# Scan outputs in pairs of heads, and a first modulation in column halves

## The chip, the cores and the metric

One program on one core of a Trainium2 chip. The metric is the device time of one execution in microseconds. The core has five instruction streams that run side by side and meet through semaphores: TensorE (PE; its weight loads are shown apart as PEld), VectorE (DVE), ScalarE (ACT), GpSimd (POOL) and SyncE (SP), which here issues all transfers. Each stream is worked off in the order in which it is written.

## The reference

Batch 1, 512 positions (S), width 1024 (D), float32. A modulated two-layer transformer is followed by a hybrid block with a Mamba-2 scan. Cut to what the change touches:

```python
cond = jax.nn.silu(c)
for i in range(2):
    mod = (cond @ ada_w[i] + ada_b[i])[:, None, :]          # ada_w[i]: 1024 x 6144
    sh1, sc1, g1, sh2, sc2, g2 = jnp.split(mod, 6, axis=-1)
    h = rmsnorm(x, norm1_g[i]) * (1.0 + sc1) + sh1
    y = sliding_window_sink_attention(h, ...)               # i = 0; stick-breaking for i = 1
    x = x + g1 * y
    h = rmsnorm(x, norm2_g[i]) * (1.0 + sc2) + sh2
    x = x + g2 * swiglu(h, w_gate[i], w_up[i], w_down[i])
...
# scan: 4 groups of 8 heads of 64, state 128, 4 chunks of 128 positions
seg = a_cum[..., :, None] - a_cum[..., None, :]
decay_in = jnp.exp(jnp.where(causal, seg, -jnp.inf))
y_diag = jnp.einsum("bcgjls,bcsgjp->bclgjp", cb[:, :, :, None] * decay_in, x_)
...
y_off = jnp.einsum("bclgn,bcgjpn,bcgjl->bclgjp", cc, prev, jnp.exp(a_cum))
return (y_diag + y_off).reshape(b, s, h, p)
```

## The kernel before

`score()` writes one list of ticks by hand, and each engine's function goes through that list and emits its part of every tick. So the list sets the order on every engine, and a wait on one engine holds back all that stands behind it there. `woven(main, side, every)` puts one step of `side` behind every `every` steps of `main`; `some(gen, n)` takes n steps.

**Dense work.** A step of `gemm` (tick `mm`) is one 128x128 block of weights times 128x512 activations. Both are split into a high and a low float32r part, so a step is three matmuls (L706, L709, L710). Weights come in units of eight blocks (512 KB): SyncE loads `raw`, ScalarE copies to `whi` (L1005), VectorE subtracts to `wlo` (L1267). This is tick `cut`, with three units in flight. With order "k" all tiles of a group go forward together, k by k; with "m" tile by tile. A tile is one PSUM bank.

**Modulation.** `mods()` gives, for each of the 12 vectors of 1024, eight ticks `fma` and a tick `modsum`. An `fma` is one VectorE pass over 128x1024 of `ada_w` (L1287, L1290), scaled by a column of `cond` and added into `modacc`. `modsum` sums over partitions on TensorE, eight matmuls with one column (L751), and VectorE adds the bias. Vector 0 is the first scale, 1 the first shift, 2 the first gate, 3 and 4 the shift and scale of the second norm. The first two are loaded whole at the start into `early` and `early2`; the others stream through three buffers (`ada`).

**Start.** Eight squares of X (ScalarE), their sum, the one-column sums `total` (L764, L767), GpSimd's power (L1668), `spread` (L776), then per k the `norm`: VectorE (L1318), ScalarE high part (L1033), VectorE low part (L1324). GpSimd works out the rotary angles (`first`, `angles`, L1639 to L1659).

**First attention.** The projection has ten output tiles: keys 8, values 9, queries 0 to 7. The order is (8, 9, 0), then (1, 2) woven with `keys`, then (3, 4), (5, 6), (7) woven with `queries`, whose side steps are the stages scores, exps, weights, turned, values of one block of one pair of heads. Each block also takes one `fma`. What is left of `queries` is worked off in `project(... "wo_a" ...)`, whose first half waits for each k of the attention output.

**Scan.** For a group g, `ssd(g)` is woven with the dense steps of the next projection tiles, one side step for every 1.2 dense ones (2 in the first group). Per head: tick `decay` (TensorE broadcasts the cumulated log decay with L953; VectorE subtracts the row's value and cuts at zero in four pieces, L1596; ScalarE takes exponentials, L1232 and L1233; VectorE multiplies by CB, L1600; GpSimd multiplies by C, L1712) and tick `output` (four matmuls for the four chunks, L962, and three with the states, L966). A head's output is 64 partitions of a bank, and a pair of heads shares the bank. Buffers SGM and EX are rings of three; `output` follows three heads behind `decay` (SKEW).

## Time and profile before

| | us |
|---|---|
| median of three runs | 2482.29 (2481.99 to 2486.51) |
| profiled execution | 2481.57 |
| its span, first to last instruction | 2479.7 |

| engine | busy, us | share |
|---|---|---|
| TensorE | 2339.0 | 94% |
| VectorE | 1271.2 | 51% |
| ScalarE | 844.1 | 34% |
| GpSimd | 184.2 | 7% |

### The profile page before, as it was taken

What the parts mean: (1) busy time and instruction counts of PE and PEld (TensorE: products, weight loads), DVE (VectorE), ACT (ScalarE), POOL (GpSimd) and SP (SyncE); (2) the same over time, 40 slices, a digit from 0 to 9 for tenths busy, and PEclk for the clock granted to TensorE, in tenths of its full rate; (3) what the DMA queues carried; (4) which work ended last, traced back from release to release, by engine and by line L of the source; (5) the groups of instructions that cost most, each with busy time, mean ns of one, the idle gap of its engine ahead of it and who ended that gap; (6) DMA issues with size and microseconds to landing.
All of it is one profiled execution on the core that took longest, in us unless ns stands there. A gap on an engine that the chain in (4) does not pass through costs nothing.

```text
span 2479.7 us, 27173 instructions
## 1 busy us (share of the span) xinstructions
PE 2339.0 (94%) x10934; PEld 1860.1 (75%) x10934; DVE 1271.2 (51%) x1889; ACT 844.1 (34%) x1324; POOL 184.2 (7%) x146
## 2 busy tenths in 40 slices
PE   3888899999999999999999999999999999999998
PEld 2556688888776667888887877866768887888886
DVE  6786555553356654333334456566754334553453
ACT  1564322122244543321332234333334322332232
POOL 7200100000100001000000001021120001000001
PEclk9998899999999999999999999999999999999999
DMA  6333255552221112222222222211112222232222
GB/s 247 128 128 111 72 185 210 184 189 85 93 69 54 58 52 77 100 96 96 100 94 77 102 85 94 100 45 60 62 66 102 95 101 85 85 99 97 86 101 77
DMA packets 70974, 250.92 MB, mean 101 GB/s; under 512 B 7872, under 2 KB 8000, under 8 KB 70848
## 3 DMA queue, kind: packets, MB, share of 16 engines
q1 hardware_dynamic: 70848, 249.17, 29.2%
q8 instruction: 87, 1.43, 0.2%
q14 instruction: 39, 0.32, 0.0%
HBM read 244.95 MB, written 4.19 MB: 100 GB/s over the span
## 4 chain that ended last, share of the span: by engine, by line
PE 84%; DVE 9%; ACT 4%; issue 2%; POOL 1%; DMA 0%; DVEq 0%; SPq 0%; POOLq 0%; ACTq 0%
PE pb L706 25%; PE pb L709 24%; PE pb L710 24%; DVE slab L1290 2%; PE pb L962 1%; DVE wlo L1267 1%; ACT whi L1005 1%; PE pb L751 1%; PE pb L966 1%; PE pb L894 1%; PE pb L869 1%; PE pb L728 1%; PE pb L729 1%; PE pb L730 1%; PE pb L879 1%
## 5 line engine op out<-in xcount | busy, mean ns | idle before, releaser
L1267 DVE TENSOR_TENSOR wlo<-raw,whi 128x1024 fp32r<-128x1024 f32 x361 | 449.8, 1248 | 766.1 <-ACT whi L1005 765.9
L706 PE MATMUL pb<-hhi,whi 128*128 128x512 f32 x1976 | 802.8, 406 | 9.4 <-ACT hhi L1033 6.2
L709 PE MATMUL pb<-hlo,whi 128*128 128x512 f32 x1976 | 777.9, 394 | 0.5 <-DVE hlo L1324 0.5
L710 PE MATMUL pb<-hhi,wlo 128*128 128x512 f32 x1976 | 776.2, 393 | 0.0
L1005 ACT ACTIVATE whi<-raw 128x1024 fp32r<-128x1024 f32 x361 | 381.0, 1057 | 848.7 <-PE pb L710 812.8
L706 PEld LDWEIGHTS pb<-hhi,whi 128*128 128x128 f32 x1976 | 374.6, 190 | 117.9 <-issue 43.7
L709 PEld LDWEIGHTS pb<-hlo,whi 128*128 128x128 f32 x1976 | 375.1, 190 | 79.9 <-DVE hlo L1324 3.8
L710 PEld LDWEIGHTS pb<-hhi,wlo 128*128 128x128 f32 x1976 | 374.1, 189 | 79.7
L706 PE MATMUL pb<-ahi,whi 128*128 128x512 f32 x848 | 337.4, 398 | 3.3 <-ACT ahi L1163 2.2
L709 PE MATMUL pb<-alo,whi 128*128 128x512 f32 x848 | 332.1, 392 | 1.1 <-DVE alo L1263 1.1
L710 PE MATMUL pb<-ahi,wlo 128*128 128x512 f32 x848 | 331.5, 391 | 0.0
L706 PEld LDWEIGHTS pb<-ahi,whi 128*128 128x128 f32 x848 | 159.8, 188 | 43.5 <-issue 7.5
L709 PEld LDWEIGHTS pb<-alo,whi 128*128 128x128 f32 x848 | 160.0, 189 | 34.9 <-DVE alo L1263 2.5
L710 PEld LDWEIGHTS pb<-ahi,wlo 128*128 128x128 f32 x848 | 160.0, 189 | 33.5
L1682 POOL TENSOR_TENSOR slab<-slab 128x512 f32<-128x512 f32 x44 | 56.7, 1289 | 1631.6 <-ACT slab L1024 1631.1
L1347 DVE SCALAR_TENSOR_TENSOR slab<-slab,vec 128x509 f32<-128x509 f32 (+2 forms) x132 | 99.0, 750 | 4.7
L1263 DVE TENSOR_TENSOR alo<-slab,ahi 128x512 fp32r<-128x512 f32 x90 | 62.9, 699 | 65.3 <-ACT ahi L1086 48.4
L1290 DVE SCALAR_TENSOR_TENSOR slab<-slab,small 128x1024 f32<-128x1024 f32 x70 | 89.4, 1278 | 1.2
L1378 DVE TENSOR_TENSOR slab<-slab,pb 128x512 f32<-128x512 f32 x66 | 45.0, 682 | 48.5 <-PE pb L710 48.5
L1024 ACT ACTIVATE slab<-X 128x512 f32<-128x512 f32 x56 | 35.4, 632 | 100.2 <-DVE X L1360 59.6
L1086 ACT ACTIVATE ahi<-slab 128x512 fp32r<-128x512 f32 x66 | 41.7, 632 | 81.6 <-DVE slab L1378 81.3
L751 PE MATMUL pb<-cst,slab 128*128 128x1 f32 x192 | 27.6, 274 | 43.8 <-DVE slab L1290 42.9
(187 smaller groups left out, 1845.5 us busy)
## 6 DMA issues: line engine op xcount, KB each, us to landing
raw<-stream SPq DMA_DIRECT2D x361, 512.0 KB, 3.3
slab<-ada_w SPq DMA_DIRECT2D x80, 512.0 KB, 4.5
early<-ada_w SPq DMA_DIRECT2D x16, 512.0 KB, 13.5
X<-xT SPq DMA_DIRECT2D x8, 256.0 KB, 6.8
ya<-slab SPq DMA_DIRECT2D x8, 256.0 KB, 2.5
slab<-ya SPq DMA_DIRECT2D x8, 256.0 KB, 4.9
outT<-X SPq DMA_DIRECT2D x8, 256.0 KB, 2.1
cst<-consts SPq DMA_DIRECT2D x1, 646.5 KB, 3.9
```

The lines of the kernel that those rows point to most:

```text
L706: e.matmul(out, wh, hi, start=s.k == 0, stop=False)
L709: e.matmul(out, wh, lo, start=False, stop=False)
L710: i = e.matmul(out, wl, hi, start=False, stop=s.last)
L751: i = e.matmul(b[:, d:d + 1], modacc[:, quarter(d)], C("one"), start=d == 0, stop=True, skip_group_check=True)
L1005: e.activation(whi[:, u % NW, :], raw[:, u % NRAW, :], ACT.Copy).then_inc(*a_cut.up(u))
L1086: e.activation(a_out[f % HALF][0], SG[f % 6], ACT.Copy).then_inc(*a_half.up(("f", l, f)))
L1263: e.tensor_tensor(out, src, hi.bitcast(F), ALU.subtract).then_inc(*v_half.up(key))
L1267: e.tensor_tensor(wlo[:, u % NW, :], raw[:, u % NRAW, :], whi[:, u % NW, :].bitcast(F), ALU.subtract).then_inc(*v_cut.up(u))
L1290: e.scalar_tensor_tensor(modacc, a, cond[:, k:k + 1], modacc, ALU.mult, ALU.add).then_inc(*v_mod.up(("fma", n)))
L1347: e.scalar_tensor_tensor(t[:, d:], u[:, :S - d], W(name, (width - 1 - d) * tiles + i), t[:, d:], ALU.mult, ALU.add).then_inc(*v_conv.up((k ...
L1378: e.tensor_tensor(t, t, b, ALU.mult).then_inc(*v_ev.up(tile))
L1682: e.tensor_tensor(acc, acc, sq_of(sid, d), ALU.add).then_inc(*p_sum.up((sid, d)))
```

## The change

It has two parts that share nothing but buffers.

**Scan.** `output` handles two heads: the matmuls of the even and of the odd head alternate, and they write the lower and the upper 64 partitions of the bank. VectorE's four pieces are gone; ScalarE takes them as four Relu of a negated difference, then waits for them and takes the exponential of the negated result. The rings are six deep, in buffers of their own (`spare`, over parts of `ahi` and `alo` that are free then), and the waits for the last state are dropped. Output pairs follow two pairs behind (SKEW = 2), and a pair counts as two side steps.

**Start.** Shift and scale of the first norm are loaded as two column halves of 512. Per k, VectorE multiplies the scale's half (tick `pre`), while TensorE sums the shift's half at once: four matmuls with the weights of `ada_w` as the stationary side and one column of `cond` as the moving one (L774). `premod` sums the scale's half (L782) and adds the biases. Norms 0 to 3 follow the first half. The first group has five tiles, and the second half is done between its steps. The constants' longest part (`late`) is loaded last. The other passes of `mods` are taken out of `queries`: nine side steps go into the first group, eighteen into the second half of `wo_a`.

```diff
@@ score
-    run(some(mod, 9))
+    for k in range(4):
+        tick("pre", 0, k)
     tick("total", 0)
     tick("scaled", 0)
-    run(some(mod, 8))
+    tick("pow", 0)
     tick("first")
-    tick("pow", 0)
+    for k in range(4, KD):
+        tick("pre", 0, k)
     tick("spread", 0)
+    tick("premod", 0)
     s.cut(0)
-    run(some(mod, 1))
-    tick("angles")
-    for k in range(KD):
+    for k in range(4):
         tick("norm", 0, k)
         if k in (1, 3):
             s.cut((k + 1) // 2)
+    tick("angles")
...
-                next(mod, None)
...
-    run(group(8, 9, 0))
+    first = group(8, 9, 0, 1, 2)
+    run(some(first, 10))
+    for ks in ((0, 1), (2, 3, 4), (5, 6, 7)):
+        for k in ks:
+            tick("pre", 1, k)
+        if ks[-1] < 7:
+            run(some(first, 5))
+    tick("premod", 1)
+    for k in range(4, KD):
+        tick("norm", 0, k)
+    run(woven(first, some_mods(9), 2))
     tick("tables")
-    run(woven(group(1, 2), keys(), 2))
+    run(woven(group(3, 4), keys(), 2))
     side = queries()
-    for ts in ((3, 4), (5, 6), (7,)):
+    for ts in ((5, 6), (7,)):
...
-        run(gemm(src, K, outs(4), "m", evac=evac))
+        last = gemm(src, K, outs(4), "m", evac=evac)
+        run(last if ahead is None else woven(last, some_mods(18), 1.5))
...
-        for hh in range(8 + SKEW):
-            if hh >= SKEW:
-                tick("output", g, hh - SKEW)
-                yield 1
-            if hh < 8:
-                tick("decay", g, hh)
-                yield 1
+        for j in range(4 + SKEW):
+            if j < 4:
+                for hh in (2 * j, 2 * j + 1):
+                    tick("decay", g, hh)
+                    yield 1
+            if j >= SKEW:
+                tick("output", g, j - SKEW)
+                yield 2
@@ tensor
+        def pre(half, k):
...
+            for d in range(4):
+                i = e.matmul(b[:, d:d + 1], a[:, quarter(d)], cond[:, k:k + 1], start=k == 0 and d == 0, stop=True, skip_group_check=True)
...
@@ scalar, decay
-            w.wait_ge(v_ssd, ("seg", g, h))
-            if n >= 3:
-                w.wait_ge(t_ssd, ("y", *divmod(n - 3, 8)))
-            w.wait_ge(t_ssd, ("state", g, 2))
+            sg, ex, b = SGM[n % 6], EX[n % 6], bank(("decay", g, h))
+            w.wait_ge(t_ssd, ("decay", g, h))
+            if n >= 6:
+                w.wait_ge(t_ssd, ("y", *divmod(n - 6, 8)))
             e.activation(ex[:, P:], b[:, P:], ACT.Exp).then_inc(*a_ssd.up(("ex", g, h)))
-            e.activation(sg, sg, ACT.Exp).then_inc(*a_ssd.up(("sg", g, h)))
+            for c in range(4):
+                o = P + 32 * c + 8 * g + h
+                m = e.activation(sg[:, quarter(c)], b[:, quarter(c)], ACT.Relu, bias=nat[:, o:o + 1], scale=-1.0)
+            m.then_inc(*a_ssd.up(("fall", g, h)))
+            w.wait_ge(a_ssd, ("fall", g, h))
+            e.activation(sg, sg, ACT.Exp, scale=-1.0).then_inc(*a_ssd.up(("sg", g, h)))
@@ sync
-        for n in range(16):
-            a = early[:, n, :] if n < HALF else early2[:, n - HALF, :]
-            e.dma_start(a, ada_in(n)).then_inc(*d_early[n].up("in"))
+        for half in range(2):
+            for k in range(KD):
+                for j in (1, 0):
+                    e.dma_start(early_part(half, k, j), io["ada_w"][0, k * P:(k + 1) * P, j * D + S * half:j * D + S * half + S]).then_inc(
+                        *d_early[half, k].up("in"))
+            if half == 0:
+                for _ in range(NRAW):
+                    load()
+        e.dma_start(cst[:, soon:], io["consts"][:, soon:]).then_inc(*d_late.up("in"))
```

The places that matter, as the built programs order them. TensorE at the program's start, before (L751 are the modulation's sums, L764 and L767 the square sums, L776 the spread, L706 to L710 a dense step):

```order
L751 MATMUL pb<-cst,slab 128x1 x8
L764 MATMUL pb<-cst,slab 128x1 x4
L767 MATMUL pb<-cst,slab 128x1 x4
L776 MATMUL pb<-cst,small 128x128 x4
L751 MATMUL pb<-cst,slab 128x1 x8
L706 MATMUL pb<-hhi,whi 128x512
```

and after (L774 is `pre`, L796 and L799 the square sums, L808 the spread, L782 `premod`, L719 to L723 a dense step):

```order
L774 MATMUL pb<-small,early 128x1 x16
L796 MATMUL pb<-cst,slab 128x1 x4
L799 MATMUL pb<-cst,slab 128x1 x4
L774 MATMUL pb<-small,early 128x1 x16
L808 MATMUL pb<-cst,small 128x128 x4
L782 MATMUL pb<-cst,slab 128x1 x4
L719 MATMUL pb<-hhi,whi 128x512
```

Sixteen matmuls of the two vectors' sums become 32 and 4, and they stand among the square sums instead of around them. VectorE at the start, before (L1287 and L1290 are the passes, L1297 and L1302 bias and gain, L1307 the square sums' scale, L1267 a split):

```order
L1287 TENSOR_SCALAR slab<-early,small 128x1024
L1290 SCALAR_TENSOR_TENSOR slab<-early,small,slab 128x1024 x3
L1290 SCALAR_TENSOR_TENSOR slab<-early_65,small,slab 128x1024 x4
L1267 TENSOR_TENSOR wlo<-raw,whi 128x1024
L1297 TENSOR_TENSOR small<-pb,vec 128x8
L1318 SCALAR_TENSOR_TENSOR slab<-X,small,pb 128x512
```

and after (L1340 and L1343 the passes, L1369 the scale, L1348 to L1351 bias and gain, L1313 a split, L1382 the norm):

```order
L1340 TENSOR_SCALAR slab<-early,small 128x512
L1343 SCALAR_TENSOR_TENSOR slab<-early,small,slab 128x512 x3
L1369 TENSOR_SCALAR small<-pb 128x4
L1343 SCALAR_TENSOR_TENSOR slab<-early,small,slab 128x512 x4
L1348 TENSOR_TENSOR small<-pb,vec 128x4
L1349 TENSOR_TENSOR small<-pb,vec 128x4
L1351 SCALAR_TENSOR_TENSOR small<-small,vec 128x4
L1313 TENSOR_TENSOR wlo<-raw,whi 128x1024
L1382 SCALAR_TENSOR_TENSOR slab<-X,small,pb 128x512
```

The passes are half as many and half as wide, and the split of the first weight unit has moved from ahead of the bias to behind it. TensorE in the scan, before, one head's output (`pb4` is the pair's bank, `slab_62` holds all buffers):

```order
L710 MATMUL pb0<-ahi_58,wlo_55 128x512
L962 MATMUL pb4<-slab_62 64x128 x2
L966 MATMUL pb4<-slab_62 64x128
L962 MATMUL pb4<-slab_62 64x128
L966 MATMUL pb4<-slab_62 64x128
L962 MATMUL pb4<-slab_62 64x128
L966 MATMUL pb4<-slab_62 64x128
```

and after, a pair's (L995 the chunks, L1001 the states; `spare3` and `spare4` are the two heads' SGM, `spare6` and `spare7` their EX):

```order
L723 MATMUL pb6<-ahi_58,wlo_55 128x512
L995 MATMUL pb5<-spare3_69,slab_62 64x128
L995 MATMUL pb5<-spare4_70,slab_62 64x128
L995 MATMUL pb5<-spare3_69,slab_62 64x128
L995 MATMUL pb5<-spare4_70,slab_62 64x128
L1001 MATMUL pb5<-spare6_72,slab_62 64x128
L1001 MATMUL pb5<-spare7_73,slab_62 64x128
```

The two heads' matmuls alternate now.

## Rows read from the trace of the kernel before

**Rows 1.** The page: groups with busy, mean ns; issues with us to landing

```profile
L1267 DVE TENSOR_TENSOR wlo<-raw,whi 128x1024 fp32r<-128x1024 f32 x361 | 449.8, 1248 | 766.1 <-ACT whi L1005 765.9
...
L1290 DVE SCALAR_TENSOR_TENSOR slab<-slab,small 128x1024 f32<-128x1024 f32 x70 | 89.4, 1278 | 1.2
...
slab<-ada_w SPq DMA_DIRECT2D x80, 512.0 KB, 4.5
```

**Rows 2.** Windows: stretch, length, busy PE PEld DVE ACT POOL, clock, DMA share, GB/s

```profile
77.00:92.00 15.00, 13.90 (x78) 10.99 (x77) 5.27 (x8) 6.41 (x11) 3.21 (x2) 1.00 0.36 122
92.00:188.00 96.00, 81.98 (x502) 52.64 (x500) 86.33 (x284) 56.54 (x174) 12.09 (x6) 0.96 0.43 143
207.00:252.60 45.60, 37.02 (x206) 23.84 (x205) 29.19 (x97) 19.72 (x59) 2.01 (x1) 0.78 0.32 105
252.60:276.30 23.70, 23.70 (x107) 19.46 (x105) 10.77 (x11) 8.56 (x11) 7.75 (x6) 1.00 0.27 90
276.30:400.00 123.70, 113.98 (x504) 94.92 (x504) 67.62 (x76) 35.98 (x44) 1.02 (x1) 0.92 0.44 157
1528.00:1850.00 322.00, 303.64 (x1480) 229.98 (x1480) 209.73 (x344) 123.47 (x187) 52.62 (x49) 0.97 0.20 68
```

**Rows 3.** Timeline of the start (start, length); first, GB/s from 14 to 34 us

```profile
GB/s 401 426 434 426 393 393 401 393 410 418 434 434 393 393 401 401 401 418 442 426 393 393 401 410 393 410 451 426 393 393 401 410 393 410 442 434 393 393 401 401
...
12.77 1.35 ACT L1024 ACTIVATE slab<-X 128x512 f32<-128x512 f32 x2 [0.24 <-DVE slab L1276]
...
29.01 3.54 PE L751 MATMUL pb<-cst,slab 128*128 128x1 f32 x16 [29.01 <-DVE slab L1290]
...
34.12 1.85 PE L767 MATMUL pb<-cst,slab 128*128 128x1 f32 x8
...
37.77 2.08 PE L776 MATMUL pb<-cst,small 128*128 128x128 f32 x8 [1.81 <-POOL small L1668]
...
53.84 0.76 PE L706 MATMUL pb<-hhi,whi 128*128 128x512 f32 x1 [1.95 <-ACT hhi L1033]
```

**Rows 4.** The same kinds at the high clock: timeline; then a group of 1530 to 1850

```profile
126.28 1.95 PE L751 MATMUL pb<-cst,slab 128*128 128x1 f32 x16 [0.90 <-DVE slab L1290]
...
254.04 0.39 PE L709 MATMUL pb<-alo,whi 128*128 128x512 f32 x1
254.26 0.39 PE L710 MATMUL pb<-ahi,wlo 128*128 128x512 f32 x1
...
L776 PE MATMUL pb<-cst,small 128*128 128x128 f32 x16 | 2.1, 274 | 0.0
```

**Rows 5.** Timeline of TensorE: outputs in the second attention, and in the scan

```profile
867.42 0.66 PE L894 MATMUL pb<-slab 128*64 128x128 f32 x8 [0.74 <-DVE slab L1525]
...
872.47 0.88 PE L894 MATMUL pb<-slab 128*64 128x128 f32 x12
873.28 0.50 PE L706 MATMUL pb<-hhi,whi 128*128 128x512 f32 x1
...
1640.69 0.65 PE L962 MATMUL pb<-slab 128*64 128x128 f32 x4
...
1642.36 0.50 PE L706 MATMUL pb<-hhi,whi 128*128 128x512 f32 x1
```

**Rows 6.** Waits of TensorE in the scan (total, times, longest); timeline of one

```profile
PE pb L962 <- DVE slab L1600: 13.2, 3, 4.4
...
1626.08 0.50 PE L953 MATMUL pb<-acR,pairR 64*128 64x512 f32 x1
...
1631.67 1.28 ACT L1232 ACT_TABLE_LOAD   x1
...
1632.96 0.49 ACT L1232 ACTIVATE slab<-pb 128x384 f32<-128x384 f32 x1
1633.35 0.62 ACT L1233 ACTIVATE slab<-slab 128x512 f32<-128x512 f32 x1
...
1634.00 1.07 DVE L1600 TENSOR_TENSOR slab<-slab 128x512 f32<-128x512 f32 x1 [1.98 <-ACT slab L1233]
```

## What the change will do to the time, and why

> **What bounds the kernel now.** I read the share of busy time first: by the table of engines TensorE is busy 94% of the span. So time is won only where TensorE waits, runs at the low clock, or streams work that could be shorter. The stretches by stage show where that is. In the first attention TensorE is busy 82 of 96 us (92 to 188), with VectorE at 90%, and 37 of 45.6 us in its tail (207 to 252.6) [rows 2]. The scan, 1528 to 1850 us, has TensorE busy 304 of 322 us. Hence two questions: when does the first dense matmul start, and what is a scan output worth?
>
> The head [rows 3]: the inputs land by 13.5 us (the last square starts at 13.49). VectorE then multiplies up two modulation vectors, 16 passes of 1.28 us or more [rows 1], and the first eight end when TensorE's sums begin, at 29.0. The other eight, TensorE's further one-column sums, the norm and the splits follow, and the first dense matmul starts at 53.84. VectorE is the chain there; the weights come at 410 GB/s, 1.28 us for 512 KB, no slower than VectorE's passes.
>
> **Head, part by part.** After the change half of the columns is enough. Per k, VectorE multiplies 512 columns and TensorE takes four one-column matmuls (two records each). The constants are 256 KB shorter, so 0.6 us earlier; the pair of k=0 lands at 13.2 - 0.6 + 1.3 = 13.9. TensorE is in order. A record of this kind takes 3.54/16 = 0.22 us there at the low clock and 1.95/16 = 0.12 later at the high one [rows 3, 4]. Its queue: 8 k x 8 records x 0.22 = 14.1; the square sums twice 1.8; the spread 2.1; the four sums of the scale 1.8. Together 21.6, so 35.5. Data are not the limit (last pair 22.9), nor is VectorE (8 passes of about 0.7). Behind it stand on VectorE three small operations (0.5 with a gap), then the split of weight unit 0, which was hidden before the modulation's end and now is not (1.2, the mean of a split [rows 1]; GpSimd begins its angles only after the first power now, and runs beside all this), then 0.75 for the norm and 0.75 for ScalarE. First dense matmul: 39.1, **14.7 us earlier**.
>
> The clock is the choice in this sum. In the trace one-column sums run almost without a gap from 29.0 to 36.0, and at 37.77 the spread still takes 2.08 us for 8 records, against 1.05 at the high clock, as 16 take 2.1 [rows 4]; the first dense matmul is long too (0.76 at 53.84, 0.39 later); the page's clock row reads high there, the durations do not. I take the low clock, 1.2 GHz. The Trainium skill (TensorE: Matmul & The Clock Gate, section on the HAM clock gate) says that sustained activity of the array releases the clock; by that rule the 21 us of sums would run at 2.4 GHz. It is the first rival; the row speaks against it.
>
> **First group and attention.** One group now has 5 tiles, 40 steps of 3 matmuls at 0.69 us (0.23 each) [rows 4], where two groups had 24 and 16. From 39.1: 10 steps, the first 4 us low, to 48; then in three pieces 36 one-column matmuls of the second half, 8 us that no other engine can hide, with 10 steps between, to 63.6; a wait of 2 us for the small operations, the norm and ScalarE; then 17 steps to 78. There stands the third modulation's sum. VectorE has four norms at 2.2 us (0.75 twice and ScalarE's 0.75 between), 8 passes (9.7) and two splits from 64 on, and the ring of three ada buffers (4.5 us from issue to landing) [rows 1] costs a little, so it is ready at 86: TensorE waits 8 us. End 91, of which 1 is low clock. Keys beside 16 steps took 15 us (77 to 92) and do again: attention starts at 106 instead of 92.
>
> Attention has 168 side steps (a stage of one pair of heads each; I counted them in the order). Before, 121 ran beside 40 dense steps and 22 passes in 96 us; the rest, 47 with 12 dense steps and 7 passes, in 45.6 us (207 to 252.6), with dense steps alone in between. Now 73 run beside 24 dense steps, and 95 beside 32 dense steps, with no pass. From [rows 2], the first stretch without passes and splits costs VectorE (86.3 - 27 - 7)/121 = 0.43 us a side step, and TensorE (82 - 28 - 4)/121 = 0.42. So the first 73: TensorE 31 + 17 = 48, VectorE 35; with the start 51, to 157. The last 95: TensorE 40 + 22, VectorE 48, if all overlapped and the clock were high: 62 us. But the tail before took (45.6 - 9)/47 = 0.78 a side step at clock 0.78, low, latency of the chain included. I take 0.75, nearer to that row since it is the same mixture: 71, to 228. Ends: 62 and 105 (all TensorE work at the low clock, less what overlaps).
>
> Then the second half of the projection gets 16 passes and two sums. It took 23.7 us with VectorE busy 10.8. VectorE now adds 14 x 1.28 + 2 x 0.75 = 19.4 and twice a wait for TensorE's 1.95: 35 us, VectorE-bound; TensorE alone would need 28. I take 35: 263 instead of 276.3. **Sum of the first part: 13.3 us less**, so of the 14.7 hardly any is lost, and little is gained by moving passes. They go beside other work in either case, in the first feed-forward block at nothing (TensorE 114 of 124 us, VectorE 68).
>
> **Scan outputs.** A head's output is 7 matmuls, 14 records, all on one column half: 1640.69 to 1642.36, 1.67 us [rows 5]. In the second attention the two heads alternate halves: 12 records take 0.81 us until the next matmul, and are busy 0.88 where 8 are busy 0.66: 0.22 for each further 4. One half alone needs 0.22 for 2 (14 in 1.67). Data and weights there have the same shapes, 128x64 and 128x128. So a pair's 28 records take 0.81 + 4 x 0.22 = 1.69 instead of 3.34; 16 pairs save **26.4 us**, all on TensorE's path.
>
> The chain that feeds it changes engine. VectorE loses four pieces (1.12 a head, 36 us in all). ScalarE gains four Relu pieces of 128 columns and a wait for their end. No row shows such a piece. From above, 0.49, the whole 384 columns; from below 0.14: 128 columns less cost 0.13 (0.62 and 0.49 at 1632.96 and 1633.35), so 0.49 - 0.26 = 0.23, and the next starts 0.1 before the end (1633.35 is 0.39 on). I take 0.2, as the shape is a third of that row's. A head: 0.39 + 0.8 + 0.15 + 0.62 = 2.0 us on ScalarE, plus 0.7 of splits and evacuations, against TensorE's 2.9 a head (half an output 0.85, decay 0.43, 2.4 dense steps). It keeps up, but not at a group's start: first decay 1626.08, ScalarE free at 1631.67, behind the two gate tiles; table load 1.28, two heads 4.0, VectorE 1.08: ready 1638.0. TensorE, after six decays and 8 steps, is there at 1634.2: a wait of 3.9. The last two pairs have no decays between them and wait some 1.5 each. About 6.5 us in three groups, 19.5, against 13.2 now [rows 6]; the first group, at two steps a piece, has no wait before or after. The wait for the last state is gone from ScalarE, since buffers are apart; the one on a state's GpSimd product stays. **Scan: 26.4 - 6.3 = 20.1 us less.**
>
> **Sum:** 2479.7 - 13.3 - 20.1 = 2446.3, and 1.9 us lie around the span (2481.57 for that run, 0.7 under the median of 2482.29): **2448**.
>
> **Rivals.**
> Early clock: the one-column sums run at 0.12, the head is paced by data (last pair 23, sum 24, spread 1.05, 0.5, then 3.5): 29, another 10 us. 2438. For it: TensorE never rests. Against: the spread at 37.77. 10%.
> Cover everywhere: ScalarE's queue and the mixture both leave no waits. The 19.5 of the scan and the 9 of attention's tail (62 for 71) go, 2420. For it: the clock fell to low three times in the scan right behind the 4.4 us waits. 17%.
> Head eaten: attention's tail goes low, as 207 to 252.6 did, its 95 side steps between 78 and 105 us: 2455 to 2482. For it: clock 0.78 there, TensorE's small matmuls alone did not raise it. 20%.
> No overlap of the halves: the scan only pays the 6.3. 2475. Against it [rows 5]. 3%.
> Slower: ScalarE bounds the scan. Each 0.1 us more a Relu piece is 3.2 us a group of 8 heads once bound. At 0.62, the row of 512 columns, a head needs 3.7 and with the rest 4.4 against 2.9: 13.5 more in each of three groups and 6 in the first, 46.5: 2495. It decides near 0.55 a piece, where three groups and a part of the first make up the 38 us that must go. 4%.
>
> **How the numbers follow.** Forecast 46%, 2448, itself from 2440 to 2455. About 0.2%, 5 us, is what a measurement of this kernel can tell. Faster by more than that takes in the forecast, the first two, no overlap and two thirds of the third (13%): 0.89. Within 0.2% (2477 to 2487) is the other third, 0.07; slower is the last, 0.04. The range leaves out the slower case, the end of the third and the far side of the second: 2420 to 2477.
>
> **What would show it.** First dense matmul at 39 (29: early clock). One-column records in the head 0.22. A wait before the third sum of the modulation of 8 us. Attention's first residual at 228, the end of the projection at 263. A pair's 28 records in 1.7 us. Relu pieces of 0.23, starts 0.2 apart. A wait before the first output of groups two to four of 4 us. Wrong would be the forecast if the Relu pieces start over 0.4 apart, or if attention's tail shows the clock below 0.7.

## The result, and the profile after

| | before | after |
|---|---|---|
| median, us | 2482.29 | 2472.17 |
| ratio, with its 95% interval | | 0.995 (0.9934 to 0.9966) |
| span of the profiled execution, us | 2479.7 | 2470.4 |
| TensorE busy, us | 2339.0 | 2333.3 |
| VectorE busy, us | 1271.2 | 1224.8 |
| ScalarE busy, us | 844.1 | 877.7 |

The change gains 10 us, where 34 were forecast. One of the five executions of the changed kernel took 2974.84 us, at a granted clock of 0.741, and is left out of the ratio.

Both kernels have the same dense steps, from the first output projection on in the same order. So I number them by the first matmul of each step (L706 before, L719 after) and compare when the same step starts. Ahead of the first attention scores stand 57 of them now instead of 41: 16 steps, 11 us at 0.69, of that row's difference have only moved. That splits the difference by stage:

| at | before | after | after minus before |
|---|---|---|---|
| first dense step | 53.84 | 37.94 | -15.9 |
| 21st dense step | 72.71 | 67.61 | -5.1 |
| first attention scores | 96.24 | 121.9 | +25.6 |
| end of the first attention | 250.45 | 250.42 | 0.0 |
| end of the output projection | 276.3 | 309.3 | +33.0 |
| first step of the feed-forward block | 287.09 | 320.20 | +33.1 |
| its 33rd step | 320.56 | 344.77 | +24.2 |
| 601st step | 622.60 | 651.66 | +29.1 |
| 1601st step, ahead of the scan's groups | 1474.79 | 1505.69 | +30.9 |
| 1951st step, behind them | 1851.19 | 1843.38 | -7.8 |
| last step | 2465.74 | 2456.36 | -9.4 |

Two large terms, of opposite sign: the start part **loses 31 us** and the scan part **gains 39**. The forecast had -13.3 and -20.1.

**The head** is as forecast. The timeline of TensorE after (start, length), to be held against [rows 3]:

```profile
13.79 6.96 PE L774 MATMUL pb<-small,early 128*128 128x1 f32 x32 [13.79 <-DMA early<-ada_w]
...
37.94 0.76 PE L719 MATMUL pb<-hhi,whi 128*128 128x512 f32 x1 [3.55 <-ACT hhi L1073]
```

32 records in 6.96 us are 0.22 each, and none of them waits: the queue of TensorE itself is the head's length now.

**The first group.** The same timeline, from the second half of the columns on:

```profile
60.62 3.09 PE L774 MATMUL pb<-small,early 128*128 128x1 f32 x24
63.69 1.87 PE L782 MATMUL pb<-cst,slab 128*128 128x1 f32 x8
67.61 0.80 PE L719 MATMUL pb<-hhi,whi 128*128 128x512 f32 x1 [2.05 <-ACT hhi L1073]
...
95.12 3.55 PE L764 MATMUL pb<-cst,slab 128*128 128x1 f32 x16 [12.13 <-DVE slab L1333]
...
99.95 0.63 PE L719 MATMUL pb<-hhi,whi 128*128 128x512 f32 x1
101.23 0.63 PE L719 MATMUL pb<-hhi,whi 128*128 128x512 f32 x1
```

VectorE's passes for it end at 95.0 us, and 5.8 us of that are waits for their transfers (before 83.69, 86.33 and 93.69). TensorE stands 12.1 us before the third modulation's sum. The sum runs at the low clock (3.55 us, against 1.95 in [rows 4]), and the first steps behind it too, 1.28 us apart instead of 0.69.

**The second half of the projection.** Windows (columns as in [rows 2]): first of after, the first attention, the second half of the projection, the norm, 33 steps of the feed-forward block:

```profile
122.00:254.50 132.50, 118.25 (x700) 75.69 (x701) 91.17 (x373) 80.95 (x248) 14.09 (x7) 0.93 0.08 26
254.50:309.30 54.80, 34.23 (x131) 28.38 (x129) 31.75 (x28) 7.59 (x10) 8.43 (x6) 0.72 0.56 192
309.30:320.20 10.90, 4.83 (x26) 4.42 (x24) 2.91 (x5) 2.41 (x3) 1.02 (x1) 0.62 0.28 96
320.20:344.80 24.60, 24.60 (x97) 19.85 (x98) 18.27 (x22) 10.51 (x13) 0.00 (x0) 0.89 0.23 80
```

and of before, the second half and the same steps of the feed-forward block:

```profile
254.50:276.30 21.80, 21.80 (x98) 17.92 (x96) 8.92 (x9) 7.61 (x10) 7.75 (x6) 1.00 0.29 97
287.10:320.60 33.50, 29.79 (x113) 24.26 (x114) 18.84 (x24) 10.51 (x13) 0.00 (x0) 0.80 0.25 94
```

With 16 passes and two sums the second half takes 54.8 us instead of 21.8. Neither engine is full in it: TensorE 34.2, VectorE 31.8. The first 33 steps of the feed-forward block get 8.9 of that back: before, a modulation's sum stood there (at 309.15 us, behind a wait of 3.7, 3.5 us long), with a low clock (0.80). By the 601st step 4.9 are lost again: the last modulation's sum now stands at 601.7 us, behind a wait of 2.2, and takes 3.1. VectorE's timeline for the first eight of these passes, TensorE's wait at their end, GpSimd's work beside them, and TensorE's waits for passes from 247 to 345 us (total, times, longest):

```profile
260.11 2.42 DVE L1333 SCALAR_TENSOR_TENSOR slab<-slab,small 128x1024 f32<-128x1024 f32 x1
263.67 1.28 DVE L1333 SCALAR_TENSOR_TENSOR slab<-slab,small 128x1024 f32<-128x1024 f32 x1 [1.13 <-DMA slab<-ada_w]
...
272.93 1.28 DVE L1333 SCALAR_TENSOR_TENSOR slab<-slab,small 128x1024 f32<-128x1024 f32 x1 [1.18 <-DMA slab<-ada_w]
...
275.85 3.58 PE L764 MATMUL pb<-cst,slab 128*128 128x1 f32 x16 [11.69 <-DVE slab L1333]
...
260.16 1.29 POOL L1736 TENSOR_TENSOR slab<-slab 128x512 f32<-128x512 f32 x1 [2.55 <-ACT slab L1064]
...
PE pb L764 <- DVE slab L1333: 20.6, 2, 11.7
```

A pass and the work between passes take 2.06 us (259.27 to 275.80 for eight), not 1.28, and TensorE has done its 14 steps at 264.2. VectorE's next pass starts only behind the sum and its bias, at 279.54.

**The scan.** ScalarE's timeline at the start of the second group, then TensorE's wait before the first output and one whole pair:

```profile
1655.30 1.28 ACT L1273 ACT_TABLE_LOAD   x1
1656.59 0.49 ACT L1273 ACTIVATE slab<-pb 128x384 f32<-128x384 f32 x1
1656.98 1.14 ACT L1276 ACTIVATE slab<-pb,slab 128x128 f32<-128x128 f32 x4
1658.15 0.63 ACT L1279 ACTIVATE slab<-slab 128x512 f32<-128x512 f32 x1
1658.68 0.47 ACT L1273 ACTIVATE spare<-pb 128x384 f32<-128x384 f32 x1
...
1661.72 0.29 PE L995 MATMUL pb<-slab 128*64 128x128 f32 x1 [2.61 <-DVE spare L1656]
...
1671.58 0.66 PE L995 MATMUL pb<-slab 128*64 128x128 f32 x8
1673.25 0.50 PE L719 MATMUL pb<-hhi,whi 128*128 128x512 f32 x1
```

A pair's 28 records take 1.67 us (1671.58 to 1673.25), where one head's 14 took 1.67 [rows 5]. A head costs ScalarE 2.08 us (1656.59 to 1658.68 for the same step). The waits before outputs sum to 8.4 us instead of 13.2, and the clock is low for 3.4 us of this stage instead of 17. Of the three waits of 2.6 (from 1659.1, 1740.1 and 1822.2 us) only the second has a stretch of low clock behind it. The terms add up: 26.4 us of matmuls, 4.8 of waits and 6.8 of clock make 38.0 of the 38.7.

### The profile page after: what moved, and what is told of

The parts are those of the page before. It is cut to its first block, busy times and chain, and to the rows that moved or that the text cites. A ratio compares the mean times of both kernels' runs of the same rounds, so it can differ in the third digit from the quotient of the medians.

```text
span 2470.4 us, 27405 instructions
## 1 busy us (share of the span) xinstructions
PE 2333.3 (94%) x11046; PEld 1862.7 (75%) x11046; DVE 1224.8 (50%) x1764; ACT 877.7 (36%) x1452; POOL 188.7 (8%) x146
## 4 chain that ended last, share of the span: by engine, by line
PE 86%; ACT 5%; DVE 5%; issue 2%; DMA 1%; POOL 1%; SPq 0%; POOLq 0%; DVEq 0%; ACTq 0%
PE pb L719 25%; PE pb L722 25%; PE pb L723 24%; DMA slab<-ada_w 1%; PE pb L764 1%; DVE wlo L1313 1%; ACT whi L1045 1%; PE pb L774 1%; PE pb L926 1%; PE pb L901 1%; PE pb L859 1%; PE pb L741 1%; DVE slab L1333 1%; PE pb L808 1%; PE pb L743 1%
## 5 line engine op out<-in xcount | busy, mean ns | idle before, releaser
L1313 DVE TENSOR_TENSOR wlo<-raw,whi 128x1024 fp32r<-128x1024 f32 x361 | 450.3, 1249 | 756.2 <-ACT whi L1045 756.1
L719 PE MATMUL pb<-hhi,whi 128*128 128x512 f32 x1976 | 800.6, 405 | 12.2 <-ACT hhi L1073 9.0
L723 PE MATMUL pb<-hhi,wlo 128*128 128x512 f32 x1976 | 777.7, 394 | 0.0
L719 PEld LDWEIGHTS pb<-hhi,whi 128*128 128x128 f32 x1976 | 375.6, 190 | 116.4 <-issue 39.5
L723 PEld LDWEIGHTS pb<-hhi,wlo 128*128 128x128 f32 x1976 | 375.2, 190 | 80.5
L719 PE MATMUL pb<-ahi,whi 128*128 128x512 f32 x848 | 338.4, 399 | 6.1 <-ACT ahi L1205 4.9
L723 PE MATMUL pb<-ahi,wlo 128*128 128x512 f32 x848 | 332.4, 392 | 0.0
L719 PEld LDWEIGHTS pb<-ahi,whi 128*128 128x128 f32 x848 | 160.6, 189 | 46.6 <-issue 8.3
L723 PEld LDWEIGHTS pb<-ahi,wlo 128*128 128x128 f32 x848 | 160.3, 189 | 33.9
L1736 POOL TENSOR_TENSOR slab<-slab 128x512 f32<-128x512 f32 x44 | 57.4, 1304 | 1647.7 <-ACT slab L1064 1647.2
L1576 DVE TENSOR_TENSOR_SCAN slab<-slab,cst 128x128 f32<-128x128 f32 (+3 forms) x64 | 52.5, 820 | 28.4 <-ACT slab L1218 28.4
```

What stands on the lines that cost most here:

```text
L719: e.matmul(out, wh, hi, start=s.k == 0, stop=False)
L723: i = e.matmul(out, wl, hi, start=False, stop=s.last)
L1313: e.tensor_tensor(wlo[:, u % NW, :], raw[:, u % NRAW, :], whi[:, u % NW, :].bitcast(F), ALU.subtract).then_inc(*v_cut.up(u))
L1576: e.tensor_tensor_scan(p[:, 0:wd][:, ::-1], RS[n % 4][:, 0:wd][:, ::-1], C("late", S - wd)[:, 0:wd][:, ::-1], 1.0, ALU.mult, ALU.max).then ...
L1736: e.tensor_tensor(acc, acc, sq_of(sid, d), ALU.add).then_inc(*p_sum.up((sid, d)))
```

## Experiments

Each kernel was timed beside the kernel before, in three rounds; medians in us, and the ratio to before with its 95% interval. "The changed kernel" is the one of the diff above.

### One part alone: scan_only and start_only

The diff above, cut to its scan part (with the six buffers of `spare`), and to its start part.

> The kernel before with the scan part of the change alone. The two traces, aligned dense step by dense step, give the scan 38.7 us. Theory A (this gain is the scan's own: 26.4 of matmuls, 5 of waits, 7 of low clock that stood behind the 4.4 us waits): 2482 - 39 = 2443, with one low-clock stretch in the scan instead of three. Theory B (the low-clock stretches fell as they did by the phase of a run, not because of the waits): they come back, 2450.

> The kernel before with the start part of the change alone. Theory A (the parts add up; the start costs what the aligned traces show up to the scan, 31 us): 2513. Theory B (part of the loss before the scan is chance of the clock, 5 us of it after 600 us): 2508 or less.

Measured: scan_only **2445.65** (0.9849, 0.9834 to 0.9864), start_only **2513.61** (1.0121, 1.0106 to 1.0136). By the runs of before beside them, the parts are -38.1 and +29.9, together -8.2, and the change itself gives -10.1: they add up. Theory A holds for both. Half of the change is slower than the kernel before, and the good half alone is the faster kernel. In scan_only the scan (1601st to 1951st step) takes 340.5 us against 376.4 before, with three short low-clock stretches of 3.4 us and the waits of 2.6 that go before them. So theory A's "one stretch instead of three" was wrong. In the changed kernel the same three waits have one stretch behind them and the scan takes 337.7: in these two kernels a wait goes ahead of every stretch, but not every wait has one behind it, and nothing in the scan's code tells the two apart. So 2.8 us of the changed kernel's gain are luck.

### Where a pass costs least: passes_beside_attention and eighteen_beside_attention

```diff
@@ queries (passes_beside_attention)
                 yield from advance()
+                next(mod, None)
@@ score, project
-    run(woven(first, some_mods(9), 2))
+    run(first)
-        run(last if ahead is None else woven(last, some_mods(18), 1.5))
+        run(last)
@@ queries (eighteen_beside_attention: the nine of the first group stay)
-        flying = []
+        flying, passes = [], some_mods(18)
                 yield from advance()
+                next(passes, None)
-        run(last if ahead is None else woven(last, some_mods(18), 1.5))
+        run(last)
```

> The changed kernel, with the passes of the other modulations back beside the first attention (one per block of a pair of heads) and neither in the first group nor in the second half of the projection. Theory A (a pass costs where TensorE has nothing else beside it; beside attention it costs 25.6 us for about 30 passes, in the second half of the projection 33 and in the first group 16): first group without its third sum ends at 86, attention begins near 102, ends near 256, projection ends at 278: 2472 - 18 = 2454. Theory B (VectorE has to do the passes somewhere and the time is the same): 2472.

> The changed kernel with the eighteen side steps of the projection's second half (16 passes, two sums) beside the attention instead, one per block, and the nine of the first group left there. Theory A (they cost 33 us in the second half and about 0.8 each beside the attention): projection's second half 22 us instead of 55, attention 14 longer, 2453. Theory B (the attention without its 16 early dense steps has no room, as with all passes there: 163 against 128 us): attention 25 longer, 2464.

Measured: **2455.08** (0.9876, 0.9855 to 0.9896) and **2454.88** (0.9884, 0.9869 to 0.99). Windows of eighteen_beside_attention, the attention and behind it the projection's second half:

```profile
117.00:271.00 154.00, 130.42 (x748) 85.01 (x747) 111.96 (x397) 83.23 (x251) 16.11 (x8) 0.90 0.24 79
271.00:292.60 21.60, 21.60 (x97) 17.73 (x96) 8.77 (x9) 7.46 (x10) 7.75 (x6) 1.00 0.29 97
```

The second half is back at 21.6 us, and from its first scores to its last values the attention takes 144.3 us against 128.6 in the changed kernel: 15.7 us for 18 side steps, 0.9 each. With 32 beside it (passes_beside_attention), the attention takes 160.2: 1.0 each. In all three the same dense steps stand beside it. In the second half of the projection the same 18 cost 33 us, 1.8 each. That is theory A, and it gives back 17 of the 31 us. Moving the nine of the first group as well brings nothing more: the attention begins 17 us sooner, at 105.7, and is 16 us longer. In passes_beside_attention the clock falls ten times in the attention (mean 0.83 from 102 to 270 us), with 56 dense steps beside it; in three_tiles below, with the same passes and 72 dense steps, it falls six times.

### Three buffers or VectorE: ring_of_five

```diff
-            a = ada[(n - 16) % 3]
+            a = ring[(n - 16) % 5]
...
-            while loaded[1] < min(96, n + 3):
+            while loaded[1] < min(96, n + 5):
```

> The changed kernel with five buffers for the modulation's weights instead of three, nothing else moved. Theory A (a pass takes 2.06 us instead of 1.28 because three buffers do not cover 4.6 us from issue to landing plus the pass): passes 1.3 apart, the two waits of 11.7 and 8.9 and the one of 12.1 each 5 to 6 us shorter, 2472 - 16 = 2456. Theory B (the passes are late because the transfers stand on SyncE's queue behind the load of a weight unit whose buffer comes free late): the waits shrink by 2 each at most, 2466 to 2472.

Measured: **2459.71** (0.9906, 0.9891 to 0.992), near theory A by the time. TensorE's waits from 247 to 310 us, the same wait of the first group, and VectorE's passes ahead of it:

```profile
PE pb L765 <- DVE slab L1334: 16.3, 2, 9.2
...
89.26 3.55 PE L765 MATMUL pb<-cst,slab 128*128 128x1 f32 x16 [7.35 <-DVE slab L1334]
...
85.05 4.06 DVE L1334 SCALAR_TENSOR_TENSOR slab<-slab,small 128x1024 f32<-128x1024 f32 x3
```

The passes wait for no transfer now (3 in 4.06 us, 1.35 each). The 12.1 us wait is 7.4, the other two together 16.3 instead of 20.6, which is less than theory A says, and the gain is 12.5 us: the attention starts 6.2 us sooner (115.7), and from its end to the feed-forward block it is 5.8 less. So the ring of three was 12 us of the loss, half in the first group and half here. The rest is VectorE's own work, standing alone behind a TensorE that has finished its few steps.

### How the early dense steps are paid for: three_tiles

```diff
-    first = group(8, 9, 0, 1, 2)
-    run(some(first, 10))
+    first = group(8, 9, 0)
+    run(some(first, 4))
...
-            run(some(first, 5))
+            run(some(first, 4))
...
-    run(woven(first, some_mods(9), 2))
+    run(first)
-    run(woven(group(3, 4), keys(), 2))
+    run(woven(group(1, 2), keys(), 2))
-    for ts in ((5, 6), (7,)):
+    for ts in ((3, 4), (5, 6), (7,)):
```

The passes stand beside the attention here too.

> The changed kernel with three tiles in the first group (the second half of the columns done between its first 12 steps), two tiles beside the keys, five beside the queries, and the passes beside the attention, as in the kernel before. Theory A (the five tiles take 16 dense steps away from the attention, where they cost little and kept the clock up; it took 163 us with them gone against 154): attention begins near 91 and takes 154, 5 to 6 us less than the scan change alone, 2440. Theory B (the 9 us by which the passes beside the attention with the new start are slower than the scan change alone are the price of the second half of the columns): 2455.

Measured: **2446.78** (0.9854, 0.9837 to 0.987), 8 us better by the medians than with five tiles (2455.08, though one of its four executions took 2446.69) and equal to scan_only (2445.65). Neither theory is right. The five tiles cost some 8 us, as A says, but the new head brings nothing even so. TensorE's timeline:

```profile
53.88 2.76 PE L775 MATMUL pb<-small,early 128*128 128x1 f32 x24
61.32 1.87 PE L783 MATMUL pb<-cst,slab 128*128 128x1 f32 x8 [4.68 <-DVE slab L1344]
65.61 0.79 PE L720 MATMUL pb<-hhi,whi 128*128 128x512 f32 x1 [2.42 <-ACT hhi L1074]
```

The first dense step is at 38.1 us, the 21st at 73.49, against 73.20 in scan_only. The 16 us of the head are spent by then: 7.3 on the second half's one-column matmuls, 1.9 and a wait of 4.7 on its sum, 2.4 on the norm, and the low clock behind. With five tiles 5.5 us of lead are left at the 21st step (67.74 in passes_beside_attention), and by the attention's end they are lost: it comes at 265.9, against 252.2 in scan_only, with the same 112 dense steps done.

### Can the head have the high clock: wide_start and wide_between

```diff
+        def fill(n):
+            b = take(("fill", n))
+            for _ in range(n):
+                e.matmul(b, hhi[:, 0, 0:P], hhi[:, 0, :], start=True, stop=True, skip_group_check=True)
+            give(("fill", n), None, None)
@@ tensor, ahead of all ticks
+        w.wait_ge(v_att, "wide")
+        fill(36)
@@ pre (wide_between alone)
+            if half == 0:
+                fill(2)
```

> The changed kernel with 36 matmuls of 512 columns on TensorE that serve nothing, before the first one-column sum, while the inputs are on their way. Theory A (one-column matmuls do not hold the clock up): the clock rises near 5 to 8 us and falls again among the sums, first dense matmul at 36 to 38, 2470. Theory B (once high it stays high while TensorE does not rest; the first rival of the prediction): one-column records at 0.12, first dense matmul at 29, 2462.

> As wide_start, with two more matmuls of 512 columns behind each k of the first half's one-column sums. Theory A (wide matmuls among them hold the clock up, one-column ones alone do not): one-column records at 0.12, sums paced by the transfers, first dense matmul near 30, 2464. Theory B (the clock is not to be had there): records at 0.22 and the wide ones 0.43 each, first dense matmul near 45, 2479.

Measured: **2474.08** (0.9959, 0.9945 to 0.9973) and **2472.45** (0.9954, 0.9939 to 0.9968), neither apart from the changed kernel's 2472. TensorE in wide_start:

```profile
1.44 11.22 PE L771 MATMUL pb<-hhi 128*128 128x512 f32 x36 [1.44 <-DVE hhi L1672]
13.78 1.02 PE L780 MATMUL pb<-small,early 128*128 128x1 f32 x8 [1.12 <-DMA early<-ada_w]
...
22.90 6.96 PE L780 MATMUL pb<-small,early 128*128 128x1 f32 x32
...
36.83 0.76 PE L719 MATMUL pb<-hhi,whi 128*128 128x512 f32 x1 [3.55 <-ACT hhi L1081]
```

and in wide_between, wide matmuls among the sums, early and later:

```profile
16.77 0.81 PE L771 MATMUL pb<-hhi 128*128 128x512 f32 x2
...
18.94 1.20 PE L771 MATMUL pb<-hhi 128*128 128x512 f32 x2
...
42.71 0.77 PE L719 MATMUL pb<-hhi,whi 128*128 128x512 f32 x1 [3.15 <-ACT hhi L1083]
```

The granted clock rises at 7.4 us, among the wide matmuls: 36 of them take 11.2 us, where all at the low clock would take 15, and the one-column records behind them run at 0.12 to 0.13. It falls at 17.6 us, among sums that stand 0.3 us apart at most, and stays low to 41.5. In wide_between, with two wide ones to eight one-column records, it falls at 17.2 (two wide ones go from 0.81 to 1.20 us) and stays low to 47.9. That settles the first rival: theory A in wide_start; in wide_between theory B for the clock, though not for the time, which it puts at 2479. Its first dense step comes 4.8 us later than the changed kernel's, and the time is the same: the first scores are 2.8 us later (124.7), and the attention takes 126.0 instead of 128.6. So here, as in three_tiles, microseconds at the head are not microseconds of the kernel.

### What the low clock behind a wait costs: wide_in_waits

```diff
             for k in range(KD):
                 tick("fma", 8 * j + k)
                 yield 1
+            if j in (2, 3, 4):
+                tick("fill", {2: 42, 3: 40, 4: 30}[j])
             tick("modsum", j)
```

> The changed kernel with matmuls of 512 columns that serve nothing on TensorE while it would wait for the sums of the modulations 2, 3 and 4: 42, 40 and 30 of them (about 9, 9 and 6.5 us at the high clock, under the waits of 12.1, 11.7 and 8.9). Nothing else is moved, so the waits' lengths stay and only the clock behind them changes. Theory A (each wait also costs the 3.5 us sum instead of 1.95 and 4 to 5 dense steps of 1.28 instead of 0.69): 4.5 us less for each of the three, 2459. Theory B (VectorE and the transfers set the pace there, and a faster TensorE only waits longer): 2466 to 2472.

Measured: **2469.51** (0.9937, 0.9919 to 0.9955), 2.7 us below the changed kernel, within what the two differ by chance. TensorE at the first of the three:

```profile
82.25 9.68 PE L773 MATMUL pb<-hhi 128*128 128x512 f32 x42
94.97 3.29 PE L766 MATMUL pb<-cst,slab 128*128 128x1 f32 x16 [3.05 <-DVE slab L1341]
98.12 0.77 PE L721 MATMUL pb<-hhi,whi 128*128 128x512 f32 x1
```

The experiment is not clean. The wide ones end 3 us before the sum can start; the clock falls again there (at 95.3 us), and the sum still takes 3.29. Only the third of the three sums, at 301.8 us, runs at the high clock (1.95). The time lies in theory B's range, but what the low clock alone costs at these waits stays open.

### Pairs or the engine of the pieces: pairs_only

scan_only, with VectorE still making the four pieces of a decay (L1596 of before), and ScalarE two exponentials.

> The kernel before with outputs in pairs and rings of six, but VectorE still making the four pieces of a decay. Scan change alone: 2446. Theory A (the 38.7 us are 26.4 of matmuls, 5 of waits and 7 of low clock, and it is the separate buffers and pairs, not the engine of the pieces, that shorten the wait at a group's start): 2446 to 2450, waits at a group's start 2.6 to 4.4. Theory B (moving the pieces to ScalarE is what shortens the chain): the waits of 4.4 and the low clock behind them stay, 2456.

Measured: **2473.66** (0.996, 0.9945 to 0.9975). My theory A is wrong, and B too small: pairs with separate buffers bring 10 us of the 38, moving the pieces to ScalarE on top of that the other 28. What moving them without pairs would bring was not run. Waits of TensorE in the scan, and a stretch of ScalarE and VectorE there:

```profile
PE pb L966 <- DVE spare L1606: 19.4, 7, 4.8
PE pb L966 <- DVE slab L1606: 9.2, 3, 4.8
...
1636.33 0.49 ACT L1239 ACTIVATE spare<-pb 128x384 f32<-128x384 f32 x1 [2.17 <-DVE spare L1602]
1636.71 0.62 ACT L1240 ACTIVATE spare<-spare 128x512 f32<-128x512 f32 x1
...
1637.37 1.07 DVE L1606 TENSOR_TENSOR spare<-spare,slab 128x512 f32<-128x512 f32 x1 [1.07 <-ACT spare L1240]
1638.36 1.11 DVE L1602 TENSOR_SCALAR spare<-pb,slab 128x128 f32<-128x128 f32 x4
...
1639.51 0.49 ACT L1239 ACTIVATE spare<-pb 128x384 f32<-128x384 f32 x1 [2.18 <-DVE spare L1602]
```

A head takes 3.18 us (1636.33 to 1639.51). VectorE's order is product of one head, then pieces of the next; so ScalarE stands 2.2 us a head for VectorE's pieces, and VectorE 1.1 for ScalarE's exponentials. The two alternate and hardly overlap. The kernel before has the same rhythm (ScalarE starts heads at 1632.96, 1636.14 and 1639.33). The matmuls saved turn into waits, 28.6 us in ten places instead of 13.2 in three. With the pieces on ScalarE a head goes through it without looking back, 2.07 us, and VectorE only follows.

### What ends the wait at a group's start: four orders

All four are scan_only with one edit.

```diff
@@ later_outputs (yield 4) and outputs_three_later (yield 3)
             if j >= SKEW:
+                if j == SKEW and g:
+                    yield 4
                 tick("output", g, j - SKEW)
@@ slower_weave
-SSD_FIRST, SSD_NEXT = 2, 1.2
+SSD_FIRST, SSD_NEXT = 2, 1.6
@@ lead_of_seven
-SSD_LEAD = 4
+SSD_LEAD = 7
```

> The scan change alone, with the first pair's output of groups two to four 4.8 dense steps later (3.3 us). Theory A (the wait of 2.6 us before it is the end of the chain through ScalarE and is covered by any work put ahead; the low clock behind it goes too): three times 2.6 and 1.7 us less, 2446 - 13 = 2433. Theory B (the wait moves to a later pair, since ScalarE's 2.07 us a head are the pace): 2446.

> The scan change alone, with 1.6 dense steps for each side step of groups two to four instead of 1.2. Theory A (more dense work between decays lets ScalarE run ahead, the waits of 2.6 shrink or go): 2446 - 8 = 2438. Theory B (the same, but the side steps reach into stretches where other work needs VectorE, or leftover ones stand alone): 2446 or more.

> The scan change alone, with the first pair's output 3.6 dense steps later instead of 4.8. In the order of the program the evacuations of a finished dense tile then stand behind the last head's decay, where with 4.8 they stood between the last two heads. Theory A (the wait of 7.8 us of the later outputs came from those evacuations and two table loads standing ahead of the last head's exponentials on ScalarE): no wait of 7.8, the one of 2.6 shrinks to 0.6 or less, 2446 - 9 = 2437. Theory B (any delay of the outputs moves the wait to a later pair): 2446 or more, with waits of 3 or more before a later pair.

> The scan change alone, with seven dense steps instead of four ahead of each group's first side step. The evacuations of a dense tile, behind which ScalarE stands at a group's start, then come three dense steps (2 us) before the first decay, and still none between the decays. Theory A (ScalarE late at the start is all that makes the wait of 2.6): wait 0.6 or less, low clock behind it gone, 2446 - 9 = 2437. Theory B (ScalarE's 2.07 us a head are the pace): a wait remains at a later pair, 2443 to 2446.

| kernel | median | ratio, interval | waits of TensorE at the scan's outputs and states |
|---|---|---|---|
| scan_only | 2445.65 | 0.9849 (0.9834 to 0.9864) | three of 2.6; 5.4 in all before states |
| later_outputs | 2463.05 | 0.9915 (0.99 to 0.9931) | three of 7.8 before the last pair; 5.4 before states |
| slower_weave | 2462.80 | 0.9912 (0.9897 to 0.9928) | 25.7 in all before states, up to 8.0 |
| outputs_three_later | **2440.14** | 0.9822 (0.9806 to 0.9839) | three of 0.6; 5.4 before states |
| lead_of_seven | 2464.50 | 0.9921 (0.9906 to 0.9936) | 27.5 in all before states, up to 8.0 |

In later_outputs the wait of 2.6 goes and one of 7.8 comes. TensorE there, and ScalarE between the seventh and the eighth head's exponentials:

```profile
1653.76 0.45 PE L968 MATMUL pb<-slab 128*64 128x128 f32 x1 [7.77 <-DVE spare L1605]
...
1643.50 1.28 ACT L1132 ACT_TABLE_LOAD   x1
...
1649.41 1.28 ACT L1241 ACT_TABLE_LOAD   x1
1650.71 0.49 ACT L1241 ACTIVATE spare<-pb 128x384 f32<-128x384 f32 x1
```

The evacuations of a finished dense tile have slipped in ahead of the last head, with two table loads: from 1643.5 to 1650.7 ScalarE does no decay. One step less of delay puts them behind it, and outputs_three_later has no 7.8, and 0.6 instead of the 2.6. That is its theory A, and the best kernel of the study, 44 us under the kernel before timed beside it (2483.85).

lead_of_seven falls to a place that neither theory named. TensorE before the first state, and GpSimd:

```profile
1626.20 2.04 PE L947 MATMUL pb<-spare,spare 128*128 128x512 f32 x2 [8.04 <-POOL spare L1707]
...
1623.80 1.26 POOL L1683 TENSOR_TENSOR slab<-slab 128x512 f32<-128x512 f32 x1 [69.47 <-ACT slab L1030]
1625.01 1.04 POOL L1707 TENSOR_TENSOR spare<-slab 128x512 f32<-128x512 f32 x1
```

Here GpSimd has the tile's sum of squares (L1683) ahead of the product of x with its decay that a state needs (L1707). The sum waits for ScalarE's square at the end of the evacuations, and TensorE waits for the product. slower_weave has the same waits at the same line (25.7 us in eight places); its three waits of 2.6 shrink to one of 1.4, as its theory A says, and this one costs more.

## Why the prediction was wrong, point by point

The forecast was 2448 with a range of 2420 to 2477; 2472.17 lies within the range, but the gain was under a third of the forecast's. The start part came out 44 us worse than forecast (+30.9 for -13.3) and the scan 19 better (-38.7 for -20.1); that two such misses end inside the range is luck. The steps that failed are the first group, the attention's tail, the projection's second half and the waits in the scan.

- **Head: right.** 39.1 forecast (its own terms add up to 38.7), 37.94 measured; one-column records at 0.22, and the choice of the low clock holds even where the clock is raised first (wide_start).
- **First group: 14 us missed.** Step: "End 91 ... attention starts at 106". By the marks that the forecast uses (the first sums of the keys and of the first queries, 77.0 and 91.9 before) it was 103.8 and 117.5. The second half of the columns was nearly right (65.6 forecast for the 21st step, 67.6 measured). Then 18 steps (the forecast says 17, but its 12.4 us are 18 of 0.69) took 15.4 us, the first four of them at the low clock; the passes ended at 95 instead of 86, held up by 5.8 us of waits for transfers; and the sum and the steps behind it took 8.7 us at the low clock, where I had 5. The keys took 13.7, where I had 15.
- **Attention: 13 us missed.** 122 forecast from its start to the first residual, 135.1 measured (117.5 to 252.6). Step: "I take 0.75 ...: 71, to 228". The 0.78 behind it was worked out with the dense steps taken off (45.6 - 9), and the 32 dense steps, 22 us, were never put back; with them it says 93. Measured were 81.0, so a side step cost 0.62 and not 0.75: two errors that partly cancel. From its first scores to its last values the attention takes 25.6 us less than before; that is the price of the passes and of 16 dense steps together.
- **Second half of the projection: the largest miss, 22 us.** Step: "35 us, VectorE-bound". From the first residual to the end it took 56.7 (252.6 to 309.3; 54.8 of them are the window above). I added VectorE's work to one length, as if it ran without a gap. In fact it runs in two rounds, and each is a chain: eight passes at 2.06 us (two more buffers save 6 us of the stage), then a sum at the low clock (3.6, with VectorE waiting for it), then steps at the low clock, and only beside those the next passes. I called the passes' cost in the feed-forward block nothing; its first 33 steps became 8.9 us shorter, of which 4.9 were lost again further on.
- "Little is gained by moving passes. They go beside other work in either case" was the sentence behind it. The runs show 1.8 us a side step in the projection against 0.9 beside the attention.
- The misses add up to the projection's end, 309.3 where 263 was forecast: -1.2 in the head, 14.0 in the first group, -1.3 in the keys, 13.1 in the attention and 21.7 in the projection are 46.3.
- **Outputs in pairs: right.** 1.69 us forecast, 1.67 measured; the rival without overlap falls.
- **Waits in the scan: wrong sign.** Step: "19.5, against 13.2 now". They are 8.4. A head's 2.0 us on ScalarE was right (2.08), and so was the chain (first output 12.0 us after the first decay, 11.9 forecast), but TensorE was there 9.4 us after the first decay, not 8.1, since a dense step between two decays takes 0.9 us; and the 1.5 us before each of the last two pairs did not come. I also charged ScalarE for the pieces, and did not ask what VectorE and ScalarE did to each other before: a head took 3.2 us through the two, and the change removes that alternation. Last, 14 us less at the low clock in this stage (about 7 us of time, 3 of them luck by scan_only) stood in no term.
- **The rivals.** "Head eaten" has the time (2455 to 2482), but by another mechanism, so that hit is luck: the last 95 side steps took 81 us, which is in its 78 to 105, but the clock of the attention's last 58 us was 0.88, not lower than the 0.78 before, and most of the loss lies ahead of it and behind it. "Cover everywhere" is near what happened in the scan (8.4 us of waits are left of the 19.5), and the opposite of what happened in the projection. "Slower" falls: the Relu pieces start 0.25 apart (1.14 for four), where I had 0.2 and that rival needed 0.55.

## What to carry to other kernels

Work that is moved off a busy stage must be costed where it lands as a chain (transfer, pass, sum, next pass), not as a sum of busy times: a stage with 22 us of dense work cannot hide two rounds of eight passes and a sum. When two engines hand one item to and fro and each is in order, look at the time from item to item (3.18 us here, for 2.2 us of work on the slower one); giving one engine both steps can be worth more than the instructions saved. And where a hand-written order is shifted by one step, look at what else stands between the shifted pieces on every engine: one dense step of delay more turned 6 us of gain into 17 of loss.

## What the hardware showed

- **TensorE's clock stayed low through the head's sums.** 32 one-column records back to back from 13.79 to 20.75 us take 0.22 each, as at 1.2 GHz, and the rest of the head, busy to 34.4, is no faster. In wide_start the clock rises to 2.4 GHz at 7.4 us, during 36 wide matmuls, and falls to 1.2 at 17.6, while such records follow each other at most 0.3 us apart. The Trainium skill (TensorE: Matmul & The Clock Gate, Part 1: The HAM clock gate) speaks of sustained busy time as what releases the clock; the rise at 7.4 us agrees, the head of the changed kernel does not, and the measurement decides.
- **A VectorE pass that starts beside a GpSimd addition takes longer.** Four of the 16 passes start with GpSimd's L1736 (1.3 to 1.5 us) or while it runs; they take 2.1 to 2.4 us instead of 1.28, in the changed kernel and in ring_of_five alike. A pass that already runs when the addition starts stays at 1.28. The product of a decay with CB takes 1.07 in pairs_only, where GpSimd's product of the same head runs beside it, and 0.69 in the changed kernel, where ScalarE's pieces lie between the two. The Trainium skill (SBUF — State Buffer, section "SBUF: two separate sides") describes a port pair that VectorE and GpSimd share and that is held for a whole instruction; these rows agree.
